# High and low halves of V as stationary operand in a written-out attention

## What is computed

```python
# per block of 128 queries, heads g, h
p_cmp = masked_softmax(q @ kc.T * scale, cmp_mask)      # 63 compressed keys
o_cmp = p_cmp @ vc
p = masked_softmax(q @ k_sel.T * scale, causal)         # 16 of 16 blocks: all keys
o_slc = p @ v_sel
p = masked_softmax(q @ kw.T * scale, window)            # the last 512 keys
o_win = p @ vw
y = g0 * o_cmp + g1 * o_slc + g2 * o_win                # gates of each query
```

## Time and profile before

| | |
|---|---|
| median of 3 runs | 1477.34 us (1473.43 to 1477.72) |
| the profiled execution | 1473.57 us, span 1471.8 us |
| busy: PE, PEld, DVE, ACT, POOL | 97%, 83%, 59%, 42%, 11% |
| granted TensorE clock over the span | 0.993 of 2.4 GHz |
| attention stage | 336.4 to 647.3 us |

### The profile page before, as it was taken

The page is one execution under the profiler, slowest core; times in us unless marked ns, Lnnn a source line. Parts: engine busy times, 40 slices in busy tenths (PEclk is TensorE's granted clock), DMA queues, the critical chain, the costliest instruction groups (busy, mean ns, idle before and its releaser), DMA issues.

```text
span 1471.8 us, 21604 instructions
## 1 busy us (share of the span) xinstructions
PE 1425.9 (97%) x7942; PEld 1222.0 (83%) x7950; DVE 872.4 (59%) x1631; ACT 621.8 (42%) x1234; POOL 161.6 (11%) x178
## 2 busy tenths in 40 slices
PE   7999999998999999998999989999999999999999
PEld 6888888877888889898987868888888788888887
DVE  3002681107767676769784486666666598569764
ACT  5014302215454545460340467755555554444441
POOL 2433343521000000000232000000000000000000
PEclk9999999999999999999999999999999999999999
DMA  5211114200000000013011014444444966643332
GB/s 176 61 47 51 51 37 121 72 7 1 1 1 1 1 1 2 1 44 115 30 51 36 30 36 165 157 151 157 157 158 137 328 206 191 211 128 100 94 114 86
DMA packets 78253, 129.41 MB, mean 88 GB/s; under 512 B 8973, under 2 KB 26826, under 8 KB 78154
## 3 DMA queue, kind: packets, MB, share of 16 engines
q1 hardware_dynamic: 77968, 128.01, 27.5%
q10 hardware_dynamic: 186, 0.08, 0.0%
HBM read 94.51 MB, written 33.55 MB: 87 GB/s over the span
## 4 chain that ended last, share of the span: by engine, by line
PE 90%; DVE 6%; ACT 2%; issue 1%; DMA 1%; SPq 0%; DVEq 0%; ACTq 0%
PE ps L519 64%; PE ps L2103 8%; PE ps L2063 4%; PE ps L2078 4%; PE ps L2123 3%; PE ps L2047 1%; PE ps L1936 1%; PE ps L2097 1%; PE ps L2068 1%; DMA x_in<-in_x_dram 1%; PE ps L758 1%; DVE hgrn_A L1600 0%; DVE hgrn_vg L1634 0%; DVE hgrn_k L1591 0%; PE ps L2168 0%
## 5 line engine op out<-in xcount | busy, mean ns | idle before, releaser
L519 PE MATMUL ps<-mlp_w_high,hidden_high 128*128 128x512 f32 x448 | 174.3, 389 | 0.0
L519 PE MATMUL ps<-mlp_w_low,hidden_high 128*128 128x512 f32 x448 | 174.3, 389 | 0.0
L519 PE MATMUL ps<-mlp_w_high,hidden_low 128*128 128x512 f32 x448 | 174.3, 389 | 0.0
L519 PE MATMUL ps<-w_high,hT_high 128*128 128x512 f32 (+1 forms) x448 | 170.5, 380 | 0.8 <-ACT cmp_v L1073 0.7
L519 PE MATMUL ps<-w_high,hT_low 128*128 128x512 f32 (+1 forms) x448 | 168.2, 375 | 0.0
L519 PE MATMUL ps<-w_low,hT_high 128*128 128x512 f32 (+1 forms) x448 | 168.0, 375 | 0.0
L2103 PE MATMUL ps<-nsa,probs_T 128*128 128x64 f32 x1056 | 138.5, 275 | 0.0
L1665 DVE TENSOR_TENSOR mlp_w_low<-mlp_w_raw,mlp_w_high 128x512 fp32r<-128x512 f32 x112 | 77.1, 691 | 98.2 <-ACT mlp_w_high L1201 98.2
L1300 ACT ACTIVATE mlp_w_high<-mlp_w_raw 128x512 fp32r<-128x512 f32 x112 | 70.6, 630 | 149.4 <-PE ps L519 149.4
L2103 PEld LDWEIGHTS ps<-nsa,probs_T 128*128 128x128 f32 x1056 | 129.2, 193 | 0.0
L1745 DVE TENSOR_TENSOR mlp_w_low<-mlp_w_raw,mlp_w_high 128x512 fp32r<-128x512 f32 x112 | 77.3, 690 | 65.7 <-ACT mlp_w_high L1300 65.7
(11 more groups left out here) (233 smaller groups left out, 2893.5 us busy)
## 6 DMA issues: line engine op xcount, KB each, us to landing
hidden_raw<-hidden_pieces SPq DMA_DIRECT2D x112, 256.0 KB, 2.7
mlp_w_raw<-in_w_mlp_in_dram SPq DMA_DIRECT2D x32, 512.0 KB, 4.2
hidden_pieces<-hidden SPq DMA_DIRECT2D x64, 256.0 KB, 2.8
mlp_w_raw<-in_w_mlp_out_dram SPq DMA_DIRECT2D x64, 256.0 KB, 4.6
w_raw<-in_w_in_dram SPq DMA_DIRECT2D x56, 256.0 KB, 2.6
hidden_pieces<-hidden_s SPq DMA_DIRECT2D x48, 256.0 KB, 2.3
x_in<-in_x_dram SPq DMA_DIRECT2D x8, 512.0 KB, 7.6
w_raw<-in_w_out_dram SPq DMA_DIRECT2D x16, 256.0 KB, 2.7
```

The lines of the kernel that those rows point to most:

```text
L519: ins = nc.tensor.matmul(out_ap, a_hl[i], b_hl[j], start=first and n == 0, stop=last and n == 2, skip_group_check=onto_a_sum_already_read)
```

## The change

Per head, slc and win outputs of two neighbouring query tiles are now made together and transposed. V is split into high and low fp32r halves once (`v_split`, written over the K and V columns of `nsa`, 128 columns for each key/value head: 64 high, 64 low) and is the stationary operand; the transposed probabilities are split into high (ACT) and low (DVE) fp32r halves and are the moving operand, 256 columns for the two query tiles. The result `[128 = high and low rows, 256 queries]` of slc and of win fills one bank, is copied by ACT to `oT` (`outputs_T_out`), transposed back on PE by four f32 transposes (`outputs_back`), copied by ACT (`rows_out`), and POOL adds the halves, multiplies by the coefficients and adds to the rows (`attention_rows`). Transposes use three banks (4, 5, 7) in rotation, outputs one (6). Every group of probabilities is now copied by ACT and, but for cmp, subtracted by DVE. The next head's `QT` is made in two halves, at items 10 and 12, after the scores. The split probabilities need room: the hgrn's v and gate rows (`hv`) are stored to DRAM as four transfers after their projection and loaded again after the attention. POOL sets tiles of zeros where a query tile has no key. Semaphores are saved: `w2_loaded` counts four chunks instead of two, and `h_loaded` reuses `x_loaded`. The diff, cut:

```diff
@@ class Items
+            if self.stacks(j):
+                self.prep.setdefault(self.stacks(j)[0], []).append(len(self.groups))
+                self.groups.append(dict(item=None, dve=True))
+            if self.returns(j) is not None:
+                self.outs.append(len(self.groups))
+                self.groups.append(dict(item=None, dve=False))
...
-                g["act"] = m % 2 == 0 or g["n"] <= 1
-                g["dve"] = not g["act"]
...
+            if g["item"] is not None:
+                g["dve"] = self.items[g["item"]][0] != "cmp"
...
+    def returns(self, j):
+        return self.ends(j - 3)
...
-PREP_AT = 9
+PREP_AT = (10, 12)
-PT_SLOTS = 10
+T_BANKS = (4, 5, 7)
@@ sync
+            for half in range(2):
+                store_hv(0, half)
             sp.wait_ge(w_used, W_OUT_AT)
             sp.dma_start(masks[:], c_masks.bitcast(BF16)).then_inc(m_loaded, 16)
             sp.dma_start(cmask[:], c_cmask.bitcast(BF16)).then_inc(m_loaded, 16)
-            sp.wait_ge(o_free, 72)
+            for half in range(2):
+                store_hv(1, half)
+            sp.wait_ge(t_full, FIRST + len(it.groups))
             sp.dma_start(tree[:, :, :].rearrange("p n t -> p (n t)"), c_tree).then_inc(t_loaded, 16)
+            sp.wait_ge(y_done, PAIRS)
+            for i in range(2):
+                sp.dma_start(hv[:, i, :, :], hv_kept[:, i, :, :]).then_inc(hv_loaded[i], 16)
...
-                    .then_inc(w2_loaded[q, c // 2], 16)
+                    .then_inc(w2_loaded[q, c // 4], 16)
@@ gpsimd
+            pool.wait_ge(hv_stored, 64)
+            for n in range(2):
+                for kind, r, c0 in (("slc", 0, 0), ("win", 0, 0), ("win", 5, P)):
+                    for x in PT[n][kind]:
+                        pool.memset(x[:, r, c0:c0 + P].bitcast(F32), 0.0).then_inc(zeroed, 1)
+            def attention_rows(n):
...
+                pool.wait_ge(t_act, FIRST + it.groups[it.outs[n]]["act_after"])
+                ys.mark(pool.tensor_tensor(u, u, o_rows[:, :, 1, :], ALU.add))
+                pool.wait_ge(coef_ready, n + 1)
+                ys.wait(pool)
+                ys.mark(pool.tensor_tensor(u4, u4, c, ALU.mult))
+                ys.wait(pool)
+                pool.wait_ge(cmp_y, h + 1)
+                ys.mark(pool.tensor_tensor(y, u4[:, 0, :, :], y, ALU.add))
+                ys.wait(pool)
+                pool.tensor_tensor(y, u4[:, 1, :, :], y, ALU.add).then_inc(y_done, 1)
@@ scalar
+            act.activation(by_head(KC0, 0), v_rows(VS0), ACT.Copy).then_inc(v_high, 1)
+            act.wait_ge(v_low, 1)
+            act.wait_ge(stage_ready, 4)
+            act.activation(by_head(KS0, 0), v_rows(VW0), ACT.Copy).then_inc(v_high, 1)
...
+            def outputs_T_out(n):
+                act.wait_ge(pv_done, n + 1)
+                if n:
+                    act.wait_ge(t_full, FIRST + it.outs[n - 1] + 1)
+                act.activation(oT[:], ps[:, O_BANK, :], ACT.Copy).then_inc(oT_out, 1)
+            def rows_out(n):
+                m = it.outs[n]
+                act.wait_ge(t_full, FIRST + m + 1)
+                if n:
+                    act.wait_ge(y_done, n)
+                act.activation(o_rows[:].rearrange("p i a d -> p (i a d)"), ps[:, t_bank(m), :], ACT.Copy).then_inc(t_act, 1)
+            act.wait_ge(hv_stored, 64)
             table_for(act, ACT.Exp)
...
             for j in range(len(it.items)):
+                high(j)
                 if it.stacks(j):
-                    prep(it.stacks(j))
...
+                    prep(*it.stacks(j))
+                if it.returns(j) is not None:
+                    rows_out(it.returns(j))
                 if j + 2 < len(it.items):
                     exponentials(j + 2)
+                if it.ends(j - 2) is not None:
+                    outputs_T_out(it.ends(j - 2))
@@ vector
+                        dve.wait_ge(t_act, FIRST + u["act_after"])
+                        dve.tensor_tensor(low, ps[:, t_bank(m), 0:u["n"] * P].rearrange("p (n t) -> p n t", t=P),
+                                          high.bitcast(F32), ALU.subtract).then_inc(t_dve, 1)
@@ tensor
             def bank_free(m):
-                u = it.groups[m - 2]
...
+                u = it.groups[m - 3]
+                pe.wait_ge(t_act, FIRST + u["act_after"])
                 if u["dve"]:
                     pe.wait_ge(t_dve, FIRST + u["dve_after"])
...
+            def outputs_T(j):
+                pe.wait_ge(t_dve, FIRST + it.groups[it.of[j][-1]]["dve_after"])
+                if kind == "slc" and n:
+                    pe.wait_ge(oT_out, n)
+                last = t if kind == "slc" else min(5, t)
...
+                for r in range(last + 1):
+                    for s, p_ in enumerate(PT[t // 2 % 2][kind]):
+                        ins = nc.tensor.matmul(o, v_split[:, t - r, v0:v0 + 2 * DK], p_[:, r, :],
+                                               start=r == 0 and s == 0, stop=r == last and s == 1)
...
+            pe.wait_ge(v_low, 2)
+            pe.wait_ge(zeroed, 12)
             for j in range(AHEAD):
                 scores(j)
             for j in range(len(it.items)):
-                if it.stacks(j):
-                    prep(it.stacks(j))
                 transposes(j)
                 if j + AHEAD < len(it.items):
                     scores(j + AHEAD)
-                if j:
-                    outputs(j - 1)
-            outputs(len(it.items) - 1)
+                if it.stacks(j):
+                    prep(*it.stacks(j))
+                if it.returns(j) is not None:
+                    outputs_back(it.returns(j))
+                if j and it.items[j - 1][0] == "cmp":
+                    cmp_outputs(j - 1)
+                elif j and it.second(j - 1):
+                    outputs_T(j - 1)
+            outputs_T(len(it.items) - 1)
+            outputs_back(PAIRS - 1)
```

More of the change, by code:

```diff
@@ L226, in stacks, with ends, pair_of, second @@
         h, k = divmod(j, self.per_head)
-        return h + 1 if k == PREP_AT and h + 1 < NH else None
-    def pair(self, j):
-        hh, k = divmod(j, self.per_head)
-        return NT * hh + (k - 1) // 2
-    def pair_end(self, n):
-        return (NT + 1) * (n // NT) + 2 + n % NT
-    def _prep(self, hh):
-        self.prep[hh] = [len(self.groups), len(self.groups) + 1]
-        for half in range(2):
-            self.groups.append(dict(item=None, hh=hh, half=half, n=4))
-PREP_AT = 9
+        return (h + 1, PREP_AT.index(k)) if k in PREP_AT and h + 1 < NH else None
+    def ends(self, j):
+        if j < 0 or self.items[j][0] != "win" or self.items[j][2] % 2 == 0:
+            return None
+        return self.pair_of(j)
+    def returns(self, j):
+        return self.ends(j - 3)
+    def pair_of(self, j):
+        kind, hh, t, _ = self.items[j]
+        return None if kind == "cmp" else NT // 2 * hh + t // 2
+    def second(self, j):
+        return self.items[j][0] != "cmp" and self.items[j][2] % 2 == 1
+PREP_AT = (10, 12)
 FIRST = 10
-PT_SLOTS = 10
 P_SLOTS = 4
@@ L250 @@
 T_BANK = 4
+T_BANKS = (4, 5, 7)
 O_BANK = 6
+PAIRS = NH * NT // 2
 A_RING = 4
@@ L633, in scores_view, with pt_slots, by_head, v_rows @@
         return ps[:, b[0], 0:w] if w <= BW else ps[:, b[0]:b[0] + 2, 0:w // 2]
[L635 to L640 removed]
+    def pt_slots(j, m):
+        kind, hh, t, tiles = it.items[j]
+        u = it.groups[m]
+        r = 1 - t % 2 + u["first"]
+        cols = slice(t % 2 * P, (t % 2 + 1) * P)
+        return [x[:, r:r + u["n"], cols] for x in PT[t // 2 % 2][kind]]
+    def by_head(c0, part):
+        return v_split[:, :, c0:c0 + 4 * DK].rearrange("p t (g a d) -> p t g a d", g=NG, a=2)[:, :, :, part, :]
+    def v_rows(c0):
+        return nsa[:, :, c0:c0 + 2 * DK].rearrange("p t (g d) -> p t g d", g=NG)
+    V_AT = {"slc": KC0, "win": KS0}
+    hv_kept = nc.dram_tensor("hgrn_v_and_gate", (P, 2, NT, HH * P), F32, kind="Internal").ap()
     def flat(ap):
```

267 lines of the change are left out of this document (144 added, 123 removed).

## The result

The changed kernel takes 1484.42 us in the median (1481.61 to 1484.68, five runs) against 1476.66 for the kernel before (1473.43 to 1477.72, five runs): 1.0068 times as long, 95% interval 1.0047 to 1.009. It is slower by 0.7% where 1.5% less was forecast, and it lies outside the range. The profiled execution took 1484.42 us with a span of 1482.6, against 1473.57 and 1471.8 before: 10.8 us more.

The account below looks back on a forecast made before the run. PE was taken to bound the kernel, idle only 9.8 of attention's 310.9 us. -117.2 + 73.0 + 12.2 - 7.5 + 12 + 4.5 + 1.4 = -21.6 us from 1473.57 gave 1452.0; predicted median 1454, range 1439 to 1474.

Parts of the forecast that it names:

- ACT and DVE: Attention stage: ACT 233 and DVE 221 us busy, under PE's 270; serial copy and subtraction stall PE +12 us (0.8 to 32).
- POOL: Attention stage: four new POOL operations per pair, 80 us in an idle engine; rows_out's wait for the previous pair's rows is covered.
- the first rival: Attention stage: ACT and DVE take turns, stalling PE 1 us per pair, 32 us instead of 12; 1474 us, chance 0.10.
- the banks bind: Attention stage: 246 groups hold three transpose banks up to 4.0 us each; stage 328 us against 283, 1499 us, chance 0.08.
- Old outputs: PE, attention: 1056 records of the old probabilities-times-V matmuls at 0.111 us each leave the path, -117.2 us.
- New outputs: PE, attention: 608 fp32r matmuls of 256 columns at 0.12 us each, +73.0 us (67.5 to 77.5).
- Transposing back: PE, attention: four f32 transposes for each of 32 pairs, 128 at 0.095 us, +12.2 us.
- Query stack: PE, attention: seven waits for the next head's stack go, -7.5 us, at worst all stay; next late: the probabilities' low half.
- Start: Ahead of PE's first score: waits for V's low halves and 12 memsets, +4.5 us (3 to 9), 1.2 for slower store or low clock.
- End: Last attention output to hgrn's first product: new chain of 3.5 us instead of 2.1, +1.4 us (1 to 3).
- hv's reload and w2's signals: After attention: 4 MB reload, nothing, up to 2 us if x1 collides; first w2 chunk waits for four loads, nothing.
- PE is busy but the stage isn't shorter than 300: Sign in the attention stage that the assumed pace of PE's matmuls is wrong, against a forecast stage of 282 to 286 us.

Follow-up runs that it names:

- the fourth experiment: Kernel before with only the next head's query stack made in two halves at items 10 and 12, behind the scores, two transpose banks: 1473.74 us, 0.9981.
- either order: Changed kernel, rows in bank 6, plus ACT's exponential ahead of the stack and row copies (1463.25 us), or PE's transposes of outputs and stack ahead of scores (1463.5 us).

## Why the prediction was wrong

**The step that failed** is the one headed "ACT and DVE": 12 us of stall, between 0.8 and 32. What stands there is sized from the work of DVE and of ACT in a pair and finds 0.4 us behind the chain of copy and subtraction. Measured are about 42 us: the 65.2 less the 18 that the kernel before has too and less 5.5 that belong to the outputs (below). The kernel before has 1.7 by the same count without its stack's wait, so some 40 were added. The exponential first, with the rows in bank 6, takes 19.2 of them back. The step never asked what stands ahead of what in ACT's queue; only under POOL did the text see that `rows_out` could hold ACT, and there for another wait. The text counted the two new copies of ACT as 0.6 us each of work; it did not read that one of them waits for a result that PE issues behind the scores, with an exponential queued behind it. The sentence that dismissed the first rival, "scores run three items ahead and exponentials two", failed with it: in the timeline the scores wait for the exponential made just before, so the real distance was one item.

That rival, "ACT and DVE take turns", was the nearest by size (32 us), but by its mechanism it was not right either. It named full engines in a serial chain; leaving out DVE's subtractions left the scores' wait at 25 us, while a new order of the same instructions took it to 2.1. The rival "the banks bind" was the only one that forecast a slower kernel, for 1499 us. Its wait was a part of what came, not the main one: PE's transposes wait 8.2 us for a bank behind DVE's subtraction, and taking the rows out of the rotation gave back 3.5 to 4 us of stalls.

**Point by point, by the sum's terms:**

- *Old outputs, -117.2.* Start to start they take 117.7 us in the stage. Right.
- *New outputs, +73.0.* 608 matmuls, start to start 78.5 us. The pace is what was forecast, the first of a run is not. The starts of one run, kernel after:

```profile
362.55 0.37 PE L2209 MATMUL ps<-probs_T_slc_high,v_high_low 128*128 128x256 f32 x1
362.75 0.28 PE L2209 MATMUL ps<-probs_T_slc_low,v_high_low 128*128 128x256 f32 x1
362.88 0.28 PE L2209 MATMUL ps<-probs_T_slc_high,v_high_low 128*128 128x256 f32 x1
362.99 0.28 PE L2209 MATMUL ps<-probs_T_slc_low,v_high_low 128*128 128x256 f32 x1
```

  The first takes 0.20, all others 0.12. 64 first ones at 0.085 more are the 5.5 us above the forecast, and 78.5 lies just above the upper bound that was given (77.5).
- *Transposing back, +12.2.* 13.5 us by the starts for the 124 in the stage, 0.109 each where 0.095 was taken. The last four stand in "The end" as well, counted twice (0.4 us). Near enough.
- *Query stack, -7.5.* The wait is gone, as forecast; its worth is not, as the fourth experiment shows, where other waits took nearly all of it. "What is late next" was asked, and the answer given was too small.
- *Start, +4.5.* +3.8 us, by the mechanism named: PE waits 5.5 us for the low half of V. The zeroed tiles, forecast for 339.9, were done at 337.5. Some 3 us more went inside the stage, by the longer low clock, for which the forecast had 1.2 with a slower store.
- *End, +1.4.* +1.2 us, a chain of 3.3 us where 3.5 was forecast.
- *POOL, hv's reload and w2's signals, nothing.* No wait on any of them is among PE's rows, in the stage or behind it. Right. POOL's own work is 70 us more, 80 forecast.
- Not in the sum: the hgrn part got 2.9 us shorter (below).

The work of PE fell by 29.0 us against 32.0 forecast, so with the stalls where they were the stage would have taken 281 us; nearly the whole miss is the stalls, +38.0 instead of +4.5. The prediction named a test for this, "PE is busy but the stage isn't shorter than 300": it is the other one that came out, a stage of 319 us with PE idle, and a row of waits (scores on the exponential) that was not on its list.

**A rule against the change.** PE's outputs start every 0.12 us, each with a weight load of its own of 0.19 us and all rows in use, so loads are hidden here. With the rule of the Trainium skill that was weighed (TensorE: Matmul & The Clock Gate, Part 3, "The mechanism": a load overlaps with matmuls in flight only when the row group differs) this trace disagrees too.

**What stays open.** With the rows in bank 6 and either order the stage is 298.4 us, where the sum gives 282.9. Of the 15.5 us between, 5.5 are the first outputs of a run, and some 10 are stalls above the 12 forecast: 46.0 less 18 and 5.5 is 22.5, of which the rows of waits above name 11.1. The rest are short waits under overlapping matmuls, which I could not assign. That the four score banks set the distance of one item is read from the program, and no run varied them. Whether a third bank would help the kernel before wasn't tried.

## What to carry to other kernels

When a change adds an instruction to an in-order queue, write down what that instruction waits for, where the other engine issues it, and what stands behind it in both queues; a copy of 0.6 us cost 17 us of stage here because an exponential stood behind it, and swapping two lines gave them back. Look-ahead in a loop counts only as far as buffers reach (here argued from the program, not varied): read from the timeline of before which item's exponential a score starts after, instead of taking the distance from the code. And a result that waits long for its reader should not sit in a rotation that others need: in a bank of its own it took 3.5 to 4 us of stalls out of the kernel after and 4 to 6 us of stage with either order, each less than the ratios of whole runs can tell from nothing.

## What the runs showed of the hardware

- **The first fp32r matmul after one of another operand type takes 0.20 us at 256 columns, the next ones 0.12**, in the starts above. It holds for the scores too, behind f32 and behind bf16: with 320 columns 0.23 against 0.15, in the kernel before. In a stage that alternates between transposes in f32, masks in bf16 and products in fp32r this comes to some 13 us in the kernel before, which looks like work.
- **DVE and POOL slow each other when both read two operands from SBUF.** Kernel after, at the end of the stage, and one POOL row from inside it:

```profile
661.53 5.84 DVE L1665 TENSOR_TENSOR hgrn_q<-hgrn_qf 128x1024 f32<-128x1024 f32 x4 [4.26 <-PE ps L2219]
662.20 1.14 POOL L1039 TENSOR_TENSOR outputs_high_low<-outputs_high_low 128x256 f32<-128x256 f32 x1 [4.95 <-ACT outputs_high_low L1237]
664.97 1.32 POOL L1045 TENSOR_TENSOR nsa<-outputs_high_low,nsa 128x128 f32<-128x128 f32 x1
362.46 0.46 POOL L1045 TENSOR_TENSOR nsa<-outputs_high_low,nsa 128x128 f32<-128x128 f32 x1
```

  DVE's four products took 5.84 us where they took 4.63 before, and POOL's additions 1.32 instead of 0.46 us. Beside DVE's subtractions inside the stage, which have one operand in PSUM, POOL kept its 0.46. The Trainium skill, SBUF — State Buffer, "SBUF: two separate sides", describes a port pair that DVE operations with two SBUF inputs and GpSimd operations reading SBUF hold in turn, each for a whole instruction; the rows agree. No cost of it shows: PE's first products waited for ACT, and the later ones wait 4.9 us for DVE in all, 6.3 before.
- **The granted clock after a pause on PE.** Six windows: two of before, three of after, and last one of the stack's part alone (columns as above):

```profile
649.20:654.00 4.80, 4.80 (x22) 4.80 (x23) 4.74 (x6) 4.77 (x7) 0.00 (x0) 0.50 0.87 311
336.40:345.70 9.30, 8.20 (x48) 7.86 (x50) 3.60 (x9) 2.78 (x11) 0.28 (x1) 0.63 0.01 2
```

```profile
663.20:668.00 4.80, 4.79 (x43) 4.80 (x44) 4.74 (x5) 4.48 (x6) 4.18 (x4) 1.00 0.20 82
654.00:663.20 9.20, 6.29 (x37) 5.72 (x38) 3.95 (x8) 3.65 (x8) 3.25 (x5) 0.81 0.08 16
340.10:354.50 14.40, 13.55 (x62) 12.29 (x63) 5.57 (x15) 4.30 (x16) 0.00 (x0) 0.50 0.01 2
```

```profile
337.70:352.10 14.40, 13.32 (x64) 12.36 (x66) 5.52 (x13) 4.17 (x15) 0.26 (x1) 0.53 0.01 2
```

  Before, the first hgrn products ran at 0.50, the 1.2 GHz level, for 4.8 us: 22 matmuls against 43 in the same length after. This is where hgrn's 2.9 us come from: its first 64 products, one group of the timeline, took 10.26 us before and 7.38 after. In the kernel after the low clock came earlier, in the gaps of the last pairs (0.81 from 654.0 on).

  At the start of the stage it stayed at 0.50 for all 14.4 us, where before the first 9.3 us averaged 0.63. The longer wait (5.5 us against 2.2) isn't shown to be the reason: with the stack's part alone PE waited the same 2.2 us as before, and the clock was at 0.53 over 14.4 us. The ninth transpose of the stage starts 10.95 us after the first score in the kernel before, 13.53 in the kernel after and 14.03 with the stack's part alone: so the longer low clock costs a stage some 3 us, and it can be part of a difference of stages above (it lasts 14.0 us of the stage's start in the kernel after, 9.6 with the rows in bank 6, 13.8 with the exponential first, 6.8 in the kernel before).

  The after stage's 0.97 is this start and 3.4 us from 654.9 on; between them it was 1.00, with PE idle 31.7 of 300.4 us. With two banks it was 0.92, by the stretches told there.
